# A two-block transformer kernel on one core: first modulation shared by VectorE and TensorE, the pool and part of the first projection moved beside the attention, and the expert choice fed from unnormed rows

## The chip, the core and the metric

The kernel runs on one core of a Trainium2 chip. The metric is the device time of one launch in microseconds (us), lower is better. Engines are named as the profile names them: PE is TensorE (PEld its weight loads), DVE is VectorE, ACT is ScalarE, POOL is GpSimd (it issues the indirect transfers here), SP is SyncE (it issues all other transfers).

## The reference, cut to what matters

Everything is float32; 256 tokens of 1024 columns, worked as two tiles (0 and 1) of 128 tokens.

```python
# first block
mod = silu(c) @ w_ada + b_ada                  # 1024 -> 6 * 1024, one row
sh_m, sc_m, gt_m, sh_f, sc_f, gt_f = split(mod, 6)
h = rms_norm(x, g_pre_mix) * (1 + sc_m) + sh_m
proj = h @ w_in                                # 1024 -> 2560: 256 pool columns, then q, k, v
pool = (banded_mean(proj[:, :256]) - proj[:, :256]) @ w_pool ...   # 4 groups of 64
attn = ...                                     # 3 dilations of 4 heads, 768 columns of q, k and v
y = concat(pool, attn) @ w_out
x = x + gt_m * rms_norm(y, g_post_mix)
h = rms_norm(x, g_pre_ffn) * (1 + sc_f) + sh_f
x = x + gt_f * rms_norm(conv_ffn(h), g_post_ffn)
# second block, twice (l = 0, 1)
x = x + mixer_l(rms_norm(x, attn_norm[l]))     # l = 0: two attentions with an index; l = 1: latent attention
h = rms_norm(x, ffn_norm[l])
q = (h @ w_q).reshape(s, 8 heads, 2, 128)      # product keys
sc = einsum(q, sub_keys)                       # 128 scores per head and half
top 16 of each half, 16 x 16 sums, top 16 of those -> 16 experts per head; g = softmax(top_s)
act = gelu(u[expert] . h)                      # rows of 1024 floats from a table of 16384
x = x + sum(g * act * v[expert])
# then a final rms_norm
```

## The kernel before, in words

`order()` writes one list of steps by hand; each engine's function walks that list and issues its own part of every step, so all queues are in order. PSUM is used as six banks in turn (`take`, L542): a step that fills a bank waits until its former reader (DVE or ACT, fixed in advance or by turns) has emptied it. Weights come through a ring of six slots of 1 MB (`weights`, L1582); a load waits until the slot's last reader is done, and all later loads wait behind it on SP.

The first modulation (`ada`, L57, L1136) works on chunks of 512 of the 6144 columns, in order 0 to 11. A chunk is two loads of 1 MB. DVE multiplies and adds its 8 blocks of 128 rows (L1146 once, L1148 seven times) into an accumulator, TensorE sums that over the partitions by a matmul with ones (`total`, L582), and DVE adds the bias, loaded as 128 copies (`finish`, L1160). Chunks 0 to 3 (sh_m and sc_m) come ahead of everything, with x, the bias of 2048 columns and the gain g_pre_mix loaded behind them. Then DVE takes the root of the mean square (`xscale`, L1174), folds 1 + sc_m with the gain (L1180), and modulates tile 0 (L1192, L1193) and, after the first 4 matmuls of the projection have been issued, tile 1. TensorE turns each tile by 8 transposes (L566), and `mm` (L605, matmul L621) multiplies: 5 column groups of `w_in`, 2 loads each, 2 tiles each. One 128x512 float32 matmul stands as two instructions in the profile. Chunks 4 to 7 lie between the steps of the projection, 8 and 9 in the attention, 10 and 11 in the up projection.

After the fifth column group comes the step `pool` (L632, L887, L1309): four band matmuls (L639), the transposes of q and k of both tiles (24 of them, L566), and the pool's matmul (L650). Then the eight attention units (`attention`, L84; 0 to 3 are tile 0, 4 to 7 tile 1): scores (L670), maximum on DVE (L1338), exp on ACT (L1020), transposes, values (L687). After the output projection (`wout`, L706), tile 0 is normed and added (`norm`, `add`, L1195, L1212), then tile 1, and then tile 0 is modulated (`modulate`, L1184) for the up projection (L753).

In the second block `choose` (L198) picks the experts of tile t in block l. The order is: sum of squares and root on ACT (L1001, L1004), Newton step and h on DVE (L1208, with the norm gain as 128 copies), 8 transposes of h (L566), 2 copies on ACT, 16 transposes of the sub-keys, then 4 column groups of w_q (L621, 8 k-steps each) with `qturn` (copy, 4 transposes, copy, score matmuls L808), and seven `pick` parts per group on DVE (L1440). ACT takes the exp of the 16 chosen scores. POOL then issues one indirect load per token tile and expert (`gather`, L1683, L1699), 512 KB each, 1024 of them, into 16 row buffers; a buffer is free when the dot product (L1537), the sum on TensorE (L825, L826) or the sum on DVE (L1556) has read it. `together` (L250) spreads the steps of the other mixers and choices between the experts by fixed costs.

Of the kernel before, what the change touches and what calls it, by code (L numbers as in the profile page):

```python
# [22 lines left out]

C_ID, C_MASK, C_FREQ, C_SGN, C_IOTA, C_END = 0, 128, 1152, 1264, 1376, 1392
# [25 lines left out]
def order():  # L50
# [6 lines left out]
    def ada():  # L57
        for i in range(12):
# [3 lines left out]
            if i not in (0, 4, 8, 10):  # L62
                put("total", i - 1)
            if i in (9, 11):
                yield
            if i in (3, 7, 9, 11):
                put("total", i)
                for n in range({3: 0, 7: 6, 9: 8, 11: 10}[i], i + 1):
                    put("finish", n)
            elif i in (5, 6):  # L70
                put("finish", i - 1)
            yield

    def projection(name, tiles):
        K, cols = PROJ[name[0]]
        for c in range(len(cols)):
            for k0 in range(0, K // 128, 4):
                for t in tiles:
                    put("mm", name, tiles, c, k0, t)
                    yield 0.85 * min(4, K // 128 - k0)  # L80
            for t in tiles:
                put("evac", name, c, t)

    def attention(name, units, cost):  # L84
        for u in range(units + 2):
            if u < units:
                put("score", name, u)
            if 1 <= u <= units:
# [7 lines left out]
    mods = ada()  # L96
    for _ in range(8):
        next(mods)
    put("xnorm")
    put("xscale")  # L100
    put("mod", "x0")
    win = projection(("win",), (0, 1))
    next(win)
    put("mod", "x1")
    put("angles")
    for n, _ in enumerate(win, 1):
        if n % 2 == 1 and n < 16:
            next(mods)
        if n == 14:
# [43 lines left out]

    def hybrid(t):
# [16 lines left out]
        yield from projection(("hyo", t), (t,))  # L171

    def mla(t):
# [22 lines left out]
        yield from projection(("mlo", t), (t,))  # L196
# [100 lines left out]
def program(nc, a, out):  # L297
    ctx = ExitStack()
    with ctx:
# [3 lines left out]
        def sem(name):  # L303
# [28 lines left out]
        l_first, l_cols, l_x, l_bias0, l_bias1, l_gains, l_tabs, l_pool, l_gains2 = (  # L332
            sem(n) for n in ("l_first", "l_cols", "l_x", "l_bias0", "l_bias1", "l_gains", "l_tabs", "l_pool", "l_gains2"))
# [14 lines left out]
        summed = sem("summed")  # L348
        held = sem("held")
# [1418 lines left out]
```

## Time and profile before

| what | us |
|---|---|
| median of 3 runs | 2113.08 |
| lowest, highest | 2112.03, 2113.08 |
| span of the profiled execution, first to last instruction | 2111.6 |

The page and the answers of the trace give the span of one execution only; the time of a run is longer than the span by what lies around the instructions, here 0.4 to 1.5 us if the profiled execution was like the timed ones. Times in rows count from the start of the span. "Idle before" in a row's brackets is the time for which the engine had nothing to do, and the arrow what ended it.

### The profile page before, as it was taken

What the parts mean: (1) busy time and instruction counts of PE and PEld (TensorE: products, weight loads), DVE (VectorE), ACT (ScalarE), POOL (GpSimd) and SP (SyncE); (2) the same over time, 40 slices, a digit from 0 to 9 for tenths busy, and PEclk for the clock granted to TensorE, in tenths of its full rate; (3) what the DMA queues carried; (4) which work ended last, traced back from release to release, by engine and by line L of the source; (5) the groups of instructions that cost most, each with busy time, mean ns of one, the idle gap of its engine ahead of it and who ended that gap; (6) DMA issues with size and microseconds to landing.
All of it is one profiled execution on the core that took longest, in us unless ns stands there. A gap on an engine that the chain in (4) does not pass through costs nothing.

```text
span 2111.6 us, 15758 instructions
## 1 busy us (share of the span) xinstructions
PE 1648.0 (78%) x4610; PEld 828.8 (39%) x4610; DVE 1375.4 (65%) x3269; ACT 388.8 (18%) x902; POOL 1128.4 (53%) x1028
## 2 busy tenths in 40 slices
PE   3997999998567978987876888878768996555565
PEld 1465887444233434432343433333434442111111
DVE  6564432142796695687757668776784887777775
ACT  1022000012121222222122222221322221100001
POOL 0000000000377577577766767776687777777773
PEclk9977999998789979999796999999788999887667
DMA  9851569162799999999999999999999999999997
GB/s 357 303 197 60 165 194 329 57 238 80 245 372 385 401 399 407 401 406 380 400 396 406 404 403 406 408 397 401 397 354 384 407 394 365 408 409 409 409 410 313
DMA packets 254483, 720.79 MB, mean 341 GB/s; under 512 B 24518, under 2 KB 49598, under 8 KB 253886
## 3 DMA queue, kind: packets, MB, share of 16 engines
q0 software_dynamic: 147456, 536.94, 65.0%
q1 hardware_dynamic: 106942, 182.85, 24.2%
q8 instruction: 38, 0.62, 0.1%
q14 instruction: 47, 0.39, 0.0%
HBM read 718.66 MB, written 1.05 MB: 341 GB/s over the span
## 4 chain that ended last, share of the span: by engine, by line
PE 40%; DMA 21%; POOL 17%; DVE 13%; issue 7%; ACT 2%; SPq 0%; POOLq 0%; DVEq 0%; ACTq 0%
POOL gring L1699 17%; DMA gring<-in_peer_v_dram,sel_idx 17%; PE PS L621 13%; PE PS L753 7%; PE PS L825 5%; PE PS L826 5%; DVE gring L1537 4%; PE PS L727 4%; PE PS L566 3%; DMA gring<-in_peer_u_dram,sel_idx 2%; DMA wring<-in_hyb_w_in_dram 1%; DVE xs L1556 1%; PE PS L670 1%; PE PS L687 1%; PE PS L706 1%
## 5 line engine op out<-in xcount | busy, mean ns | idle before, releaser
L1699 POOL DMA_INDIRECT gring<-in_peer_u_dram,sel_idx x512 | 566.0, 1105 | 725.1 <-DVE sel_g L1523 556.2
L825 PE MATMUL PS<-gring,diags 128*128 128x512 f32 x736 | 449.0, 695 | 321.3 <-DMA gring<-in_peer_v_dram,sel_idx 211.5
L1699 POOL DMA_INDIRECT gring<-in_peer_v_dram,sel_idx x512 | 562.2, 1098 | 230.3 <-issue 130.5
L1537 DVE CUSTOM_DVE_ANT_0 gring<-gring,hs 128x1024 f32<-128x1024 f32 x400 | 482.1, 1221 | 134.3 <-DMA gring<-in_peer_u_dram,sel_idx 133.1
L826 PE MATMUL PS<-gring,diags 128*128 128x512 f32 x736 | 434.2, 676 | 0.0
L621 PE MATMUL PS<-wring,hTs 128*128 128x512 f32 (+3 forms) x968 | 410.4, 574 | 9.8 <-DVE hTs L1125 4.3
L825 PEld LDWEIGHTS PS<-gring,diags 128*128 128x128 f32 x736 | 135.4, 210 | 545.4 <-issue 383.4
L621 PEld LDWEIGHTS PS<-wring,hTs 128*128 128x128 f32 x968 | 179.8, 195 | 219.8 <-issue 217.4
L826 PEld LDWEIGHTS PS<-gring,diags 128*128 128x128 f32 x736 | 158.8, 216 | 210.5 <-issue 210.5
L1063 ACT ACTIVATE diags<-consts,acts 128x128 f32<-128x128 f32 x368 | 136.4, 397 | 511.3 <-PE PS L826 476.8
L1537 DVE CUSTOM_DVE_ANT_0 gring<-gring,PS 128x1024 f32<-128x1024 f32 x112 | 136.4, 1220 | 70.4 <-DMA gring<-in_peer_u_dram,sel_idx 70.4
L753 PE MATMUL PS<-hTs,wring 128*128 128x256 f32 (+1 forms) x768 | 154.8, 365 | 1.9 <-DVE hTs L1101 1.9
L753 PEld LDWEIGHTS PS<-hTs,wring 128*128 128x128 f32 x768 | 137.5, 193 | 19.8 <-issue 2.3
L1556 DVE SCALAR_TENSOR_TENSOR xs<-gring,acts,xs 128x1024 f32<-128x1024 f32 x80 | 102.6, 1282 | 8.3 <-DMA gring<-in_peer_v_dram,sel_idx 8.1
L566 PE MATMUL PS<-consts,work 128*128 128x128 f32 (+1 forms) x344 | 67.2, 321 | 50.0 <-ACT work L1020 18.6
L950 ACT ACTIVATE work<-PS 128x512 f32<-128x512 f32 (+4 forms) x122 | 55.7, 463 | 222.0 <-PE PS L621 114.0
L1556 DVE SCALAR_TENSOR_TENSOR PS<-gring,acts,PS 128x1024 f32<-128x1024 f32 x62 | 79.9, 1288 | 12.3 <-DMA gring<-in_peer_v_dram,sel_idx 8.8
L566 PEld LDWEIGHTS PS<-consts,work 128*128 128x128 f32 (+1 forms) x344 | 48.5, 161 | 84.5 <-ACT work L1020 23.6
L1020 ACT ACTIVATE work<-work,small 128x128 f32<-128x128 f32 (+3 forms) x72 | 35.3, 490 | 226.2 <-DVE small L1345 226.2
L1148 DVE SCALAR_TENSOR_TENSOR gring<-wring,small,gring 128x512 f32<-128x512 f32 x84 | 63.1, 751 | 3.9 <-DMA wring<-in_w_ada_dram 1.1
L727 PE MATMUL PS<-gring,keep 128*128 128x512 f32 x120 | 55.0, 600 | 0.9 <-issue 0.9
L1338 DVE CUSTOM_DVE_ANT_0 work<-PS,consts 128x128 f32<-128x128 f32 (+1 forms) x72 | 25.5, 354 | 38.1 <-PE PS L670 37.4
(194 smaller groups left out, 1188.9 us busy)
## 6 DMA issues: line engine op xcount, KB each, us to landing
wring<-in_peer_w_q_dram SPq DMA_DIRECT2D x32, 1024.0 KB, 14.7
wring<-in_w_ada_dram SPq DMA_DIRECT2D x24, 1024.0 KB, 9.7
wring<-in_w_up_dram SPq DMA_DIRECT2D x44, 512.0 KB, 5.1
wring<-in_hyb_w_in_dram SPq DMA_DIRECT2D x20, 1024.0 KB, 8.3
wring<-in_w_in_dram SPq DMA_DIRECT2D x10, 1024.0 KB, 8.1
wring<-in_hyb_w_out_dram SPq DMA_DIRECT2D x8, 1024.0 KB, 19.2
gring<-in_peer_u_dram,sel_idx POOLq DMA_INDIRECT x512, 12.9
gring<-in_peer_v_dram,sel_idx POOLq DMA_INDIRECT x512, 13.4
```

Source lines behind the costliest of these rows:

```text
L566: ins = pe.e.transpose(ps[0:c, 128 * i:128 * i + 128], s, ident)
L621: ins = pe.e.matmul(ps, lhs(k), slot[s][:, k - k0, 0:n], start=(k == 0), stop=(k == kt - 1))
L727: ins = pe.e.matmul(ps, gT[:, k, 128 * t:128 * t + 128], slot[s][:, k % 4, :], start=(k == first), stop=(k == last))
L753: ins = pe.e.matmul(PS[:, 512 * b + 256 * j + c0:512 * b + 256 * j + c0 + n], slot[s][:, k % 4, off + 128 * j:off + 128 * j + 128], hT[:, ...
L825: pe.e.matmul(ybank[0], d, row[i % NG][:, 0:512], start=first, stop=last)
L826: pe.e.matmul(ybank[1], d, row[i % NG][:, 512:1024], start=first, stop=last).then_inc(summed, 1)
L950: return ac.e.activation(dst, src, ACT.Copy)
L1063: ac.e.activation(d, ident, ACT.Copy, scale=acts[:, c:c + 1]).then_inc(diag_ready, 1)
L1148: ins = e.scalar_tensor_tensor(ac, slot[s][:, k % 4, :], cact[:, k:k + 1], ac, ALU.mult, ALU.add)
L1537: e.tensor_tensor_reduce(row[i % NG], row[i % NG], hbank if (l, t) == (1, 1) and hd else h[t], 1.0, 0.0, ALU.mult, ALU.add, acts[:, c:c + ...
L1556: e.scalar_tensor_tensor(x[t] if in_x or (hd, j) == (7, 15) else vbank, row[i % NG], acts[:, c:c + 1], x[t] if in_x or (hd, j) == (0, 1) e ...
L1699: gp.e.indirect_dma_start(out=row[i % NG], out_offset=None, in_=table, in_offset=bass.IndirectOffsetOnAxis(ap=sel_idx[:, c:c + 1], axis=0) ...
```

## The change

1. The modulation's first four chunks are taken in the order 2, 3, 0, 1 (`ADA`). For these four, DVE takes rows 0 and 1 of each load's four blocks of 128 (2 of 4), and TensorE takes the other two as matmuls with the activated c broadcast over 128 columns (`cwide`), with the bias as a matmul of one row, all in the bank into which `total` adds DVE's part. The copies of the bias for these chunks are not loaded; one row of 8 KB is (`brow`).
2. Chunks 2 and 3 are multiplied with the gain straight from PSUM (`widen`), x is scaled with them, and the shift of chunks 0 and 1 is added from PSUM by halves (`shift`); each half of each tile is turned at once (`wT`), and a matmul waits for its half only.
3. `pool` is split into `pm`, `qk` and `py`. Only `qk` of tile 0 stands ahead of the attention; `pm`, `qk` of tile 1, the fifth column group of `w_in` for tile 1, and `py` stand in units 0 to 4.
4. Tile 0's modulation for the up projection stands ahead of tile 1's norm and add; both its copies go to ACT.
5. In `choose`, x itself is turned (`xT`), its first half already inside the mixer's output projection, and multiplied by the norm gain (a column per partition now) on the way out of PSUM. The w_q matmuls start without the norm; the root 1/rms goes into the exp's scale. The norm stands behind the first `qturn`, three quarters of the key transposes too.

```diff
+ADA = (2, 3, 0, 1, 4, 5, 6, 7, 8, 9, 10, 11)
     def projection(name, tiles):
+            now = tiles[:1] if (name[0], c) == ("win", 4) else tiles
...
-    mods = ada()
-    for _ in range(8):
-        next(mods)
+    for i in (2, 3):
+        for part in (0, 1):
+            put("ada", i, part)
+        put("total", i)
+        put("widen", i)
     put("xnorm")
     put("xscale")
-    put("mod", "x0")
+    for part in (0, 1):
+        put("ada", 0, part)
+    put("total", 0)
+    for t in range(2):
+        put("shift", 0, t)
+        put("wT", 0, t)
+    for part in (0, 1):
+        put("ada", 1, part)
+    put("total", 1)
+    for t in range(2):
+        put("shift", 1, t)
+    mods = ada()
     win = projection(("win",), (0, 1))
-    next(win)
-    put("mod", "x1")
+    for t in range(2):
+        next(win)
+        put("wT", 1, t)
...
-    put("pool")
-    for n, _ in enumerate(attention(("a1",), 8, 1.0)):
-        if n % 2 and n < 10:
+    put("qk", 0)
+    beside = {0: [("pm",)], 1: [("qk", 1)], 2: [("mm", ("win",), (0, 1), 4, 0, 1)],
+              3: [("mm", ("win",), (0, 1), 4, 4, 1), ("evac", ("win",), 4, 1)], 4: [("py",)]}
+    for n, _ in enumerate(attention(("a1",), 8, 1.0, beside)):
+        if n in (3, 4, 5, 7, 9):
             next(mods)
...
-                 ("sq", "y1"), ("norm", "y1"), ("add", "y1")):
+                 ("sq", "y1"), ("mod", "f0"), ("norm", "y1"), ("add", "y1")):
         put(*step)
-    put("mod", "f0")
...
+    def out_projection(name, t, l):
+        for n, units in enumerate(projection(name, (t,)), 1):
+            if n == 3:
+                put("xT", t, l, 0)
+            yield units
...
     def choose(t, l):
-        put("sq", f"c{t}{l}")
-        yield 2.0
-        put("norm", f"c{t}{l}")
-        yield 2.0
-        put("hT", f"c{t}{l}")
-        yield 1.0
-        put("hTe", f"c{t}{l}")
-        yield 1.0
-        put("keys", t, l)
...
                 put("mm", ("wq", t, l), (t,), g, k0, t)
                 yield 3.4
+                if (g, k0) == (0, 0):
+                    put("sq", f"c{t}{l}")
+                    put("xT", t, l, 1)
+                    put("keys", t, l, 0)
+                    yield 2.0
...
             put("qturn", t, l, g)
+            if g == 0:
+                put("norm", f"c{t}{l}")
+                for part in (1, 2, 3):
+                    put("keys", t, l, part)
+                yield 3.0
...
+            def ada(i, g):
+                if i >= 4:
+                    return
+                if g == 0:
+                    b, ps = take(("total", i), "vec")
+                    pe.wait_ge(l_brow, 16)
+                    pe.wait_ge(wide_ready, 1)
+                    pe.e.matmul(ps, ones[0:1, :], brow[:, 512 * i:512 * i + 512], start=True, stop=False)
...
+                for k in (2, 3):
+                    pe.e.matmul(PS[:, 512 * b:512 * b + 512], cwide[:, 2 * g + k - 2, :], slot[s][:, k, :], start=False,
+                                stop=False)
...
+            def xturn(t, l, half):
+                key, at = ("xT", t, l, 4 * half), 24 + 8 * l + 4 * half
+                ps = arrived(key)
+                freed(key, e.tensor_tensor(
+                    hT[:, 4 * half:4 * half + 4, 128:256], ps.rearrange("p (b q) -> p b q", q=128),
+                    norm_cols[:, at:at + 4].unsqueeze(2).to_broadcast([128, 4, 128]), ALU.mult))
...
+                mine = range(4) if i >= 4 else range(2)
...
+            def widen(i):
+                ps = arrived(("total", i))
+                ve.wait_ge(l_gain0, 16)
+                freed(("total", i), e.scalar_tensor_tensor(mod[:, 512 * i:512 * i + 512], ps, 1.0,
+                                                           gain[0][:, 512 * (i - 2):512 * (i - 2) + 512],
+                                                           ALU.add, ALU.mult))
+
+            def shift(half, t):
+                ps = arrived(("total", half))
+                so_far()
+                ht = h[t][:, 512 * half:512 * half + 512]
+                ins = e.tensor_tensor(ht, ps, ht, ALU.add)
...
-                ve.wait_ge(*done(e.scalar_tensor_tensor(sc_m, sc_m, 1.0, gain[0], ALU.add, ALU.mult)))
...
+                for t in range(2):
+                    done(e.scalar_tensor_tensor(h[t], x[t], norm_small("x")[7][:, t:t + 1], sc_m, ALU.mult, ALU.mult))
...
-                    ac.e.activation(ga, ga, ACT.Exp).then_inc(gate_exp, 1)
+                    ac.wait_ge(h_ready, h_n[f"c{t}{l}"])
+                    ac.e.activation(ga, ga, ACT.Exp, scale=root(t, l)).then_inc(gate_exp, 1)
...
             def ada(i, g):
                 weights(("ada", i, g), [(0, a["w_ada"][0], 512 * g, 4, 512 * i, 512)])
                 if (i, g) == (3, 1):
                     group(l_x, (x[0], a["x"][0, 0:128, :]), (x[1], a["x"][0, 128:256, :]))
-                    group(l_bias0, (mod[:, 0:2048], a["b_ada"][0, 0:2048].partition_broadcast(128)),
-                          (gain[0], a["g_pre_mix"][0].partition_broadcast(128)))
+                    group(l_gain0, (gain[0], a["g_pre_mix"][0].partition_broadcast(128)))
```

Of the three new or changed functions named `ada`, the first is TensorE's, the one with `mine` is VectorE's, the last is SP's; `xturn` as shown is VectorE's. The load group of (3, 1) is thus issued after four weight loads now, and after eight before. The tables of the rotary angles are loaded behind the first load of `w_in`.

## Rows read from the trace of the kernel before

**Rows 1.** the page: the span, and GB/s in 40 slices of it

```profile
span 2111.6 us, 15758 instructions
...
GB/s 357 303 197 60 165 194 329 57 238 80 245 372 385 401 399 407 401 406 380 400 396 406 404 403 406 408 397 401 397 354 384 407 394 365 408 409 409 409 410 313
```

**Rows 2.** busy by engine per stretch (us, count in brackets), clock, DMA share, GB/s

```profile
120.80:139.70 18.90, 16.42 (x102) 13.55 (x102) 13.42 (x51) 7.17 (x16) 0.00 (x0) 0.84 0.38 119
139.70:171.00 31.30, 31.15 (x117) 24.77 (x117) 19.94 (x63) 7.89 (x15) 0.00 (x0) 0.55 0.32 96
556.70:1000.00 443.30, 354.42 (x974) 166.03 (x974) 342.11 (x944) 100.58 (x231) 322.46 (x281) 0.91 1.01 390
1530.00:1800.00 270.00, 215.20 (x557) 97.91 (x556) 201.46 (x529) 63.27 (x144) 209.54 (x181) 0.94 1.00 381
```

**Rows 3.** chain of waits, opening and projection: start, length, what

```profile
20.17 13.85 DMA gains<-in_g_pre_mix_dram
34.11 2.48 DVE gring L1160 x4
...
41.78 1.98 PE PS L566 x8
44.62 5.47 PE PS L621 x8
...
51.84 24.27 PE PS L621 x56
...
91.56 13.73 PE PS L621 x32
```

**Rows 4.** timeline of the opening, all engines: start, length, what, idle before

```profile
2.43 0.33 SPq L1592 DMA_DIRECT2D keep<-in_attn_norm_dram  x1
...
8.74 0.49 DVE L1146 TENSOR_SCALAR gring<-wring,small 128x512 f32<-128x512 f32 x1 [3.23 <-DMA wring<-in_w_ada_dram]
9.26 5.48 DVE L1148 SCALAR_TENSOR_TENSOR gring<-wring,small,gring 128x512 f32<-128x512 f32 x7
...
14.80 2.07 PE L582 MATMUL PS<-gring,keep 128*128 128x512 f32 x2 [9.66 <-DVE gring L1148]
...
30.25 1.06 ACT L963 ACTIVATE hs<-xs 128x1024 f32<-128x1024 f32 x1 [26.34 <-DMA xs<-in_x_dram]
...
39.19 1.28 DVE L1192 SCALAR_TENSOR_TENSOR hs<-xs,small,gring 128x1024 f32<-128x1024 f32 x1
```

**Rows 5.** the stretches of the attention where the clock falls, columns as in Rows 2

```profile
129.00:134.00 5.00, 3.09 (x27) 2.61 (x26) 4.50 (x23) 1.79 (x5) 0.00 (x0) 0.96 0.01 2
134.00:167.00 33.00, 32.43 (x114) 26.12 (x113) 22.62 (x79) 7.92 (x17) 0.00 (x0) 0.50 0.32 96
```

**Rows 6.** timeline between output and up projection

```profile
192.02 0.16 DVE L1167 TENSOR_TENSOR small<-small 128x1 f32<-128x1 f32 x1
...
196.38 1.28 DVE L1192 SCALAR_TENSOR_TENSOR hs<-xs,small,gring 128x1024 f32<-128x1024 f32 x1
...
198.97 1.97 PE L566 MATMUL PS<-consts,hs 128*128 128x128 f32 x8 [8.61 <-DVE hs L1193]
```

**Rows 7.** chain of waits, first choice

```profile
517.73 0.70 DVE xs L1283
...
523.80 5.38 PE PS L566 x24
529.18 7.12 PE PS L621 x16
...
538.32 1.17 PE PS L808 x8
...
556.70 1.07 POOL gring L1699
```

**Rows 8.** the page's group of dot products, busy and mean ns

```profile
L1537 DVE CUSTOM_DVE_ANT_0 gring<-gring,hs 128x1024 f32<-128x1024 f32 x400 | 482.1, 1221 | 134.3 <-DMA gring<-in_peer_u_dram,sel_idx 133.1
```

**Rows 9.** one line's instructions: the gain multiply of the mixers, ns min/median/max

```profile
L1125 DVE TENSOR_TENSOR hTs<-PS,small x12: 674/691/692, 411.3 to 1439.7; 128x512 f32<-128x512 f32 x12
```

More of the change, by code:

```diff
@@ L57, in ada @@
     def ada():
-        for i in range(12):
+        for i in range(4, 12):
             put("ada", i, 0)
@@ L76, in projection, with attention @@
         for c in range(len(cols)):
+            now = tiles[:1] if (name[0], c) == ("win", 4) else tiles
             for k0 in range(0, K // 128, 4):
-                for t in tiles:
+                for t in now:
                     put("mm", name, tiles, c, k0, t)
                     yield 0.85 * min(4, K // 128 - k0)
-            for t in tiles:
+            for t in now:
                 put("evac", name, c, t)
-    def attention(name, units, cost):
+    def attention(name, units, cost, beside={}):
         for u in range(units + 2):
@@ L87, in attention @@
                 put("score", name, u)
+            for step in beside.get(u, ()):
+                put(*step)
             if 1 <= u <= units:
@@ L170, in hybrid @@
         put("obT", "hy", t)
-        yield from projection(("hyo", t), (t,))
+        yield from out_projection(("hyo", t), t, 0)
     def mla(t):
@@ L463, in program @@
                 loads.append((("mm", s[1], s[3], s[4]), 1))
-            elif s[0] == "keys":
-                loads.append((s, 1))
+            elif s[0] == "keys" and s[3] == 0:
+                loads.append((s[0:3], 1))
             elif s[0] == "wout":
@@ L684, in value @@
                     ready(("mm", ("hyi", t), 6, t))
+                if name[0] == "a1" and u % 4 == 0:
+                    for c in (3, 4):
+                        ready(("mm", ("win",), c, t))
                 b, ps = take(("value", name, u), "vec")
@@ L797, in keys @@
                 kv = wring[:, 2048 * s:2048 * s + 2048].rearrange("p (b c) -> p b c", b=16)
-                turn(("ky", t, l), [kv[:, i, :] for i in range(16)], "act")
-                w_free[("keys", t, l)] = (full[use[("ky", t, l, 12)][0]], use[("ky", t, l, 12)][1])
+                b, ps = take(("ky", t, l, 4 * part), "act")
+                for i in range(4):
+                    ins = pe.e.transpose(ps[:, 128 * i:128 * i + 128], kv[:, 4 * part + i, :], ident)
+                ins.then_inc(full[b], 1)
+                if part == 3:
+                    w_free[("keys", t, l)] = (full[b], use[("ky", t, l, 12)][1])
             def qturn(t, l, g):
@@ L1034, in index, with keys @@
                     freed(("index", t, g), ac.e.activation(q, ps[:, 0:nk], ACT.Relu))
-            def keys(t, l):
-                turned(("ky", t, l), 16, lambda i0, n: kyT[:, i0:i0 + n, :])
+            def keys(t, l, part):
+                key = ("ky", t, l, 4 * part)
+                ps = arrived(key)
+                freed(key, copy(kyT[:, 4 * part:4 * part + 4, :], ps.rearrange("p (b q) -> p b q", q=128)))
             def qturn(t, l, g):
@@ L1566, in expert @@
                     ins.then_inc(y_added, 1)
-            own = {"start": start, "ada": ada, "finish": finish, "xnorm": xnorm, "xscale": xscale, "norm": norm, "add": add,
+            own = {"start": start, "ada": ada, "finish": finish, "widen": widen, "shift": shift, "xnorm": xnorm, "xscale": xscale, "norm": norm, "add": add,
                    "angles": angles, "score": score, "value": value, "fold": fold, "up": up, "gfold": gfold,
@@ L1571, in vector_engine @@
             first = {"mod": modulate, "turn": attturn, "lin": mrope_key}
-            own.update({"columns": columns, "hTe": hturn_gain, "lin": linturn})
-            after = {"evac": evac, "pool": pool}
+            own.update({"columns": columns, "hTe": hturn_gain, "lin": linturn, "xT": xturn})
+            after = {"evac": evac, "py": py}
             for s in steps:
```

180 lines of the change are left out of this document (116 added, 64 removed).

## The prediction

> **What bounds the kernel now.** I read the page first: in the last three quarters of the span the transfers run at about 400 GB/s in every slice [rows 1]. The stretches say the same: from 556.70, where POOL issues its first indirect load [rows 7], the DMA share is 1.00 to 1.01 at 381 to 390 GB/s, with no engine full [rows 2]. So 1555 of 2111.6 us are bound by bytes which the change leaves alone, and an engine's time saved there is worth nothing by itself. All that comes ahead of 556.70 runs at a third or half of that rate [rows 1]: there the transfers wait for the work, and a microsecond saved starts the gathers a microsecond earlier. A gain of the change must be found there.
>
> Second, the chain of waits of the opening [rows 3]. The end of the modulation is set by the load of the gain, landed at 34.02; the adds and the modulation follow, tile 0 is turned at 41.78, the first matmul of the projection starts at 44.62, and the ninth only at 51.84, since tile 1 had to be modulated and turned in between. From there TensorE is the bound up to 120.8. In the attention it stays so: 16.42 busy of 18.90 us, then 31.15 of 31.30 [rows 2]. The clock granted from 134 to 167 is 0.50, the level of 1.2 GHz, after 5 us in which TensorE was busy for 3.09 [rows 5].
>
> Third, the first choice: from the last add at 517.73 to the first gather at 556.70 one thing follows another [rows 7].
>
> **The opening.** Loads land in the order of issue and by bytes: the first MB at 8.74 [rows 4], the gain at 34.02 [rows 3] as the end of 11.0 MB (8 weight loads of 1.05, x 1.05, bias 1.05, gain 0.52); that is 9.96 MB in 25.3 us, 0.394 MB per us. Now two small loads more stand in front, 0.35 us each by the nearest row [rows 4], and the gain ends 5.77 MB: 8.74 + 0.7 + 4.72 / 0.394 = 21.4. x ended before it here too (30.25) [rows 4]. The last weight load, (1, 1), lands at 32.0.
>
> DVE's share of a chunk falls from 0.5 + 7 x 0.785 = 6.0 to 2.9 us [rows 4]. But widen(2) needs the gain and stands ahead of chunk 3 in DVE's queue, so all behind it waits until 21.4. Then in turn: widen 0.8, chunk 3 2.9, total 2.07 (TensorE has had nothing for some 4 us, so I take the pair at the slow level [rows 4]), widen 0.8: 28.0. Mean square, root and Newton step 1.3 (36.59 to 39.19, less one product of 128x1024 [rows 3, 4]), two scalings of 1.3 [rows 4], chunk 0 2.9: 34.8. Total 1.0, two shifts of 0.7, turning the second 0.6: 37.8. Only now, as `wT` stands ahead of it in TensorE's queue, chunk 1: bias, 4 k-steps, total, 6 x 0.86 at 2.4 GHz (32 instructions in 13.73, two to a matmul [rows 3]): 43.0. The first matmul starts there, against 44.62; the weights of `w_in`, the next MB behind (1, 1), land at 34.7 and are no bound. The ninth instruction starts after 3.43 and a turning of 0.5, at 46.9 against 51.84. **4.9 us** won. The relief of DVE is real but mostly lost to the wait for the gain and to chunk 1 behind the turnings. The one-row bias matmul is in no row; it costs between nothing and the slow pair (2.07), I take 0.86 as its columns are those of any pair. The broadcast copies (2 x about 0.4) lie before 8.74.
>
> The Trainium skill (DMA: Bandwidth & Descriptors, "Queues, rings and completion order") says that completion is not FIFO per issuing engine. By that the gain could land beside x, up to 1.05 / 0.394 = 2.7 us earlier, and the sum would be 2088.8. The rows show landing in order, so it stays out of the sum.
>
> **Projection and attention.** The fifth column group of tile 1, 16 instructions or 6.9 us, leaves the projection and enters units 2 and 3. TensorE's sum over projection and attention is unchanged but for the idle time that it fills: 18.90 - 16.42 = 2.5 us [rows 2]. Against it, the turning of q and k now stands right behind the ropes and chunk 7 on DVE, which had 13.7 us of matmuls for cover and now 6.9: I price a wait of 1.0. DVE's own load in the attention grows by the pool's four small operations (1.7 us); with 13.42 of 18.90 and 19.94 of 31.30 busy it has room. Then the clock: dense matmuls in units 2 and 3 put off the fall which came at 134, and what of tile 0 ran slow may run at full: between 0 and 2.7 us for the 5.4 us from 134 to 139.7; I take 1.0. Unknown from both sides: if the moved matmuls themselves run at 1.2 GHz they cost 6.9 more; if units 4 to 7 ran at 2.4 GHz, TensorE's 31.15 would halve and DVE's 19.94 plus the pool's be the bound, some 8 us less. Sum 4.9 + 2.5 - 1.0 + 1.0 = **7.4 us** at the end of the attention.
>
> **Tile 0's modulation.** DVE has ended tile 0's Newton step at 192.18 and starts L1192 at 196.38, behind tile 1's norm and add [rows 6]. Moved ahead, TensorE's turning at 198.97 starts **4.2 us** earlier. Tile 1's norm and add move behind it by 2.5 us; its own turning is needed at the end of the first up step (9 us later), which covers them. Both copies on ACT instead of one: 0.6 behind the other, under the second half of the turning.
>
> **The first choice.** Before: add 517.73 to 518.43, squares, root, Newton, h, turning and keys from 523.80 (5.38), 16 instructions at 529.18 (7.12: part of them slow), copies and turning, scores from 538.32 to 539.49 [rows 7]. Now: the first half of x is turned inside the output projection (0.4 more on TensorE: 518.1). The first 8 instructions follow at once, the clock still up: 3.4, to 521.5. Turning of the second half 0.5, gain product 0.7 [rows 9], beside which lie the first 4 key transposes: 522.8. 8 instructions 3.4, then copy, turning, copy and scores as before (529.18 + 7.12 = 536.30 to 539.49, 3.2): 529.4. **10.0 us** won. The square, the table load and the root on ACT lie beside the first matmuls, the Newton step and h (2.5 us on DVE) beside the second and the copies; 12 key transposes beside DVE's picks. The exp takes the root as a scale, ready by 525. From the scores to the gather nothing changes (17.2 us).
>
> **The other three choices** lie in the stretch bound by bytes: nothing. There ACT loses 1.2 us of copies and DVE gains 1.4 each; the gathers' reserve covers it.
>
> **Sum.** 7.4 + 4.2 + 10.0 = 21.6 us: a span of 2111.6 - 21.6 = 2090.0. The median of the runs is 1.5 above that span, so the time is 2113.1 - 21.6 = **2091.5**.
>
> **The rivals.**
> *The clock stays low (0.11).* TensorE in the opening is fed in bursts of two k-steps and waits for each load. If it works at 1.2 GHz until 50, chunk 0's part ends after DVE's (27.2 + 8.6 + 2.1 = 37.9), chunk 1's six pairs take 10.3: the first matmul at 50, the ninth 10 us later than I say. With the moved matmuls partly slow (3.4) it gives 2105. For it: pairs of 2.07 all through the opening [rows 4], 33 us at 0.50 though busy [rows 5]. Against: of the 8 instructions in 5.47 us half already ran at full [rows 3]. The Trainium skill (TensorE: Matmul & The Clock Gate, "HAM oscillation") describes this rule: short bursts between waits for loads start slow every time. Rows 5 agree in part: the fall came after small work, with only short waits.
> *The attention speeds up (0.12).* Units 4 to 7 run mostly at 2.4 GHz: 8 us less, 2083.
> *The gathers profit too (0.07).* Slower stretches such as 1530 to 1800 (381 against 410 GB/s) hold choices; if earlier scores fill half of that, 9 us less: 2082.
> *Given back (0.09).* What the weight loads moved ahead of 556.70 they must now move behind it: at about 200 GB/s for 17 us of the gain, 3.4 MB or 8.5 us: 2100. Against: the ring of six slots is freed by the same matmuls, which come earlier too.
> *No measurable change (0.04).* Clock and giving back together: 2105 + 5 and more, near 2110.
> *Slower (0.05).* In the gathers' stretch TensorE's queue now meets DVE's three times in a choice (product of half 0, add and product of half 1) where it met it once (h); each may stand behind four dot products of 1.22 us [rows 8], and TensorE's sums, which free the row buffers, stand behind. Two more meetings at 4.9 us in three choices are 29 us; over 21.6 it decides, from 3.6 us a meeting. Time 2121. Against: 16 rows of 0.52 MB are 20 us of cover, and DVE is busy for 342 of 443 us.
>
> **How the numbers follow.** My own case has 0.52, with 2086 to 2097 by its bounds. All but the clock's, the unchanged and the slower case (0.20 together) lie between 2078 (the fast ones with the 2.7 of the gain and a little more) and 2103. What can be told from no change is 0.2%, 4.2 us, here. Faster 0.52 + 0.11 + 0.12 + 0.07 + 0.09 = 0.91, same 0.04, slower 0.05.
>
> **What would show it.** First matmul of the projection near 43 and the ninth near 47, DVE idle before the first widen until about 21; end of the values near 163.5; up projection near 190 instead of 201.9; first POOL load near 535; from there to the end 1555 again. I am wrong if the opening's pairs keep 2.07 after 30, if the clock digit in the moved matmuls is 5, or if the stretch behind the first gather is longer than 1560.

## The result, and the profile after

| | kernel before | kernel after |
|---|---|---|
| median of the first comparison, us | 2112.03 (5 runs, 2107.78 to 2113.08) | 2101.59 (5 runs, 2096.72 to 2102.72) |
| ratio, 95% interval | | 0.9948, 0.9930 to 0.9966 |
| mean of more runs, us | 2112.6 (74 runs, beside the experiments) | 2098.7 (11 runs, those five and six more) |
| profiled execution: time, span, us | span 2111.6 | 2096.72, span 2094.9 |

The change makes the kernel faster, by 10.4 us in the first comparison and by 13.9 us between the means of all runs. The forecast was 21.6 us. The same kernel spreads over some 10 us from run to run here (standard deviation 2.6 to 5.5 us), so means of many runs are used below, with one standard error behind a ±. In every run the time is 1.7 to 1.9 us above its span, 1.8 in what follows; the forecast had taken 1.5 for this.

The page after, the rows of [rows 1]:

```profile
span 2094.9 us, 15823 instructions
...
GB/s 339 307 198 61 221 179 292 115 182 116 301 397 383 401 401 403 401 406 401 395 395 407 400 404 406 369 391 401 399 382 399 408 364 363 410 409 410 409 410 308
```

The gathers' plateau begins about half a slice of 52 us earlier and looks as before. The opening, which answers to [rows 3], in the chain of waits (start, length, what):

```profile
9.41 11.91 DMA gains<-in_g_pre_mix_dram
...
21.45 0.69 DVE gring L1276
...
24.95 2.07 PE PS L638 x2
27.02 2.00 PE PS L624 x2
29.02 6.18 PE PS L629 x8
35.21 0.87 PE PS L638 x2
...
36.17 0.70 DVE hs L1284
...
36.92 1.25 PE PS L604 x8
38.17 1.05 PE PS L624 x2
39.22 3.63 PE PS L629 x8
42.85 0.86 PE PS L638 x2
43.71 3.43 PE PS L702 x8
...
47.58 3.44 PE PS L702 x8
```

Three readings: the gain lands at 21.32 instead of 34.02, and DVE does its first `widen` at 21.45; TensorE works at the slow level of its clock from 24.95 (2.07 for a pair of instructions) to about 35, though the prediction had given the slow level to one pair only; and chunk 1 (L624, L629, L638) stands between the first turnings and the first matmul of the projection (L702). The attention and the first choice, which answer to [rows 2] and [rows 7]; first the windows (busy us of PE, PEld, DVE, ACT, POOL with counts, then clock, DMA share, GB/s), then the chain:

```profile
120.80:139.70 18.90, 17.33 (x89) 11.68 (x87) 10.51 (x36) 3.53 (x8) 0.00 (x0) 1.00 0.65 222
139.70:171.00 31.30, 26.06 (x95) 19.49 (x96) 19.49 (x53) 7.21 (x13) 0.00 (x0) 0.62 0.33 102
```

```profile
510.82 0.70 DVE hTs L1240
511.66 3.69 PE PS L702 x8
...
517.36 1.17 PE PS L897 x8
518.55 0.90 DVE work L1583 x4
...
535.75 1.07 POOL gring L1826
```

Set beside the forecast:

| landmark, us | before | forecast | after |
|---|---|---|---|
| first matmul of the projection | 44.62 | 43.0 | 43.71 |
| ninth | 51.84 | 46.9 | 47.58 |
| tile 0 turned for the up projection | 198.97 | 187.4 | 187.31 |
| first POOL load | 556.70 | 535.1 | 535.75 |
| from there to the end | 1554.9 | 1555 | 1559.2 |

So the time in front of the gathers was forecast within 1 us, 21.0 measured against 21.6 (21.4 by the mean of two profiles). What is missing is missing behind them. By the mean of the runs the stretch behind is 2098.7 - 1.8 - 535.3 (mean of two profiles) = 1561.6 us for the kernel after and 2112.6 - 1.8 - 556.7 = 1554.1 for the one before: **7.5 us longer**, with a standard error of 1.3 from the runs alone and what one profile's start of the gathers may be off besides. The windows of the two stretches:

```profile
535.75:2094.90 1559.15, 1168.08 (x2854) 519.97 (x2854) 1139.46 (x2653) 310.24 (x730) 1135.40 (x1024) 0.87 1.01 392
```

and of the kernel before:

```profile
556.70:2111.60 1554.90, 1166.32 (x2854) 519.58 (x2854) 1136.62 (x2647) 311.76 (x736) 1128.21 (x1024) 0.87 1.01 393
```

Time by rate gives 611 MB on both sides. The only column that grows by more than 3 us is POOL's, by 7.2 us for the same 1024 instructions. Part of that is spread between executions: a second profile of the kernel after has 3.8 us less of both, stretch and POOL.

```profile
534.90:2090.30 1555.40, 1165.61 (x2854) 517.89 (x2854) 1139.62 (x2653) 310.14 (x730) 1131.63 (x1024) 0.88 1.01 393
```

### The profile page after: what moved, and what is told of

It is laid out like the page before. It is cut to its first block, busy times and chain, and to the rows that moved or that the text cites. A ratio compares the mean times of both kernels' runs of the same rounds, so it can differ in the third digit from the quotient of the medians.

```text
span 2094.9 us, 15823 instructions
## 1 busy us (share of the span) xinstructions
PE 1660.3 (79%) x4650; PEld 829.5 (40%) x4650; DVE 1364.9 (65%) x3261; ACT 386.4 (18%) x895; POOL 1135.6 (54%) x1028
## 3 DMA queue, kind: packets, MB, share of 16 engines
HBM read 717.63 MB, written 1.05 MB: 343 GB/s over the span
## 4 chain that ended last, share of the span: by engine, by line
PE 39%; DMA 19%; POOL 18%; DVE 14%; issue 8%; ACT 1%; SPq 0%; POOLq 0%; DVEq 0%; ACTq 0%
POOL gring L1826 18%; PE PS L702 12%; DMA gring<-in_peer_v_dram,sel_idx 12%; PE PS L838 7%; DMA gring<-in_peer_u_dram,sel_idx 5%; PE PS L914 5%; PE PS L915 4%; DVE gring L1661 4%; PE PS L812 4%; PE PS L604 2%; DMA wring<-in_hyb_w_in_dram 1%; DVE xs L1680 1%; PE PS L752 1%; PE PS L791 1%; PE PS L772 1%
## 5 line engine op out<-in xcount | busy, mean ns | idle before, releaser
L1826 POOL DMA_INDIRECT gring<-in_peer_u_dram,sel_idx x512 | 566.6, 1107 | 702.7 <-DVE sel_g L1647 535.3
L1826 POOL DMA_INDIRECT gring<-in_peer_v_dram,sel_idx x512 | 568.8, 1111 | 228.6 <-issue 126.9
L702 PE MATMUL PS<-wring,hTs 128*128 128x512 f32 (+3 forms) x968 | 411.4, 575 | 10.6 <-DVE hTs L1198 4.4
L702 PEld LDWEIGHTS PS<-wring,hTs 128*128 128x128 f32 x968 | 180.6, 196 | 221.9 <-issue 219.0
L1044 ACT ACTIVATE work<-PS 128x512 f32<-128x512 f32 (+2 forms) x123 | 56.2, 465 | 229.1 <-PE PS L702 92.9
L1258 DVE SCALAR_TENSOR_TENSOR gring<-wring,small,gring 128x512 f32<-128x512 f32 x68 | 51.1, 751 | 3.6 <-DMA wring<-in_w_ada_dram 1.5
## 6 DMA issues: line engine op xcount, KB each, us to landing
gring<-in_peer_u_dram,sel_idx POOLq DMA_INDIRECT x512, 11.7
```

The lines of the kernel that those rows point to most:

```text
L702: ins = pe.e.matmul(ps, lhs(k), slot[s][:, k - k0, 0:n], start=(k == 0), stop=(k == kt - 1))
L1044: return ac.e.activation(dst, src, ACT.Copy)
L1258: ins = e.scalar_tensor_tensor(ac, slot[s][:, k, :], cact[:, 4 * g + k:4 * g + k + 1], ac, ALU.mult, ALU.add)
L1826: gp.e.indirect_dma_start(out=row[i % NG], out_offset=None, in_=table, in_offset=bass.IndirectOffsetOnAxis(ap=sel_idx[:, c:c + 1], axis=0) ...
```

## The experiments

Each is timed beside the kernel before on the same chip. "Head" is the start of the first POOL load in its profile.

**The kernel after, again.** No edit.

> The changed kernel once more, on the chip of the next three. Its first profile had the first gather 20.9 us earlier and the end 16.7 us earlier than the kernel before, but the medians differ by only 10.4 us. If the stretch behind the first gather is truly longer, this run is again 9 to 12 us faster than the kernel before (ratio 0.994 to 0.996) with the first gather at 535 to 536 and 1559 us or more behind it. If the first comparison was unlucky, the ratio is 0.990 and the stretch 1555.

Median 2097.58, ratio 0.9931 (0.9912 to 0.9951), mean 15.1 ± 1.9 below the kernel before, head 534.90. The two theories are not parted by it: the ratio lies between theirs, and in its own profile the stretch behind the head is 1555.4 us, what "unlucky" asked for, but that execution took 2092.07 us, and by the mean of the six runs, 2097.4, the stretch is 1560.7. A part of the first comparison's shortfall was spread; by the means, not all.

**Parts undone or done alone.** Three kernels: the kernel after with the new choice only for the first one (tile 0, block 0), of whose edit the main lines come first below; the kernel after with no new choice at all (`NEW = ()`); and the kernel before with tile 0's modulation moved and nothing else (the last lines).

```diff
+NEW = ((0, 0),)
-            if n == 3:
+            if n == 3 and (t, l) in NEW:
                 put("xT", t, l, 0)
...
     def choose(t, l):
+        if (t, l) not in NEW:
+            put("sq", f"c{t}{l}")
...
-                 ("sq", "y1"), ("norm", "y1"), ("add", "y1")):
+                 ("sq", "y1"), ("mod", "f0"), ("norm", "y1"), ("add", "y1")):
```

> The changed kernel, with the new order of the expert choice for tile 0 of block 0 only; the three later choices in the old order, with normed rows. The first gather must stay at 535 to 536. Theory L (what is lost behind the first gather is lost in the reordered later choices: products and turnings between the w_q matmuls, the keys' load behind the first w_q load): the stretch behind it is 1555 again and the time 2091 to 2093, ratio 0.990. Theory H (a part of any gain ahead of the first gather is given back behind it): as fast as the changed kernel, 2100 to 2102, ratio 0.995. Theory N (no loss, it is spread between runs): 2091 to 2102 with no clear difference from the changed kernel.

> The changed kernel with all four choices in the old order: only the opening, the pool and attention, and the modulation of tile 0 are changed. From my own sum the first gather is at 545.5 (the choice's 10.0 us are gone, of 20.9). Theory L: all of the 10.9 us arrive, 2101 to 2102, ratio 0.995, so as fast as the whole change. Theory H: half arrives, 2106 to 2107, ratio 0.9975.

> The kernel before with one step moved: tile 0's modulation for the up projection ahead of tile 1's norm and add. My price is 4.2 us: the turning at 194.8 instead of 198.97, the first gather at 552.5. If a microsecond ahead of the gathers counts in full: 2107.8 to 2108.8, ratio 0.998. Theory H: 2110, ratio 0.999. If the 4.2 us are taken back by tile 1's turning (late because its norm and add now stand behind), the first gather stays at 556.7.

| kernel | head | head against 556.70 | mean time against before | ratio (interval) |
|---|---|---|---|---|
| later choices as before | 536.41 | -20.3 | -16.1 ± 2.1 | 0.9930 (0.9914, 0.9946) |
| no new choice | 545.02 | -11.7 | -6.4 ± 1.2 | 0.9969 (0.9955, 0.9983) |
| tile 0's modulation only | 553.72 | -3.0 | -4.8 ± 1.4 | 0.9978 (0.9963, 0.9992) |

The first choice counts in full: from the second row to the first the head gains 8.6 us and the time 9.7 ± 2.2. So does the moved modulation, within its error. The order in the three later choices makes no difference that these runs can tell (-16.1 and -15.1). But between the last two rows lie 8.7 us of head and only 1.6 ± 1.8 us of time: what the opening and the part beside the attention win seems to be lost again.

**Whose turn it is to copy.** Copies out of PSUM without a fixed engine go to ACT, and every fourth to DVE. The change takes six banks fewer by turns ahead of the second block, so this turn falls on other copies behind it. The counter is set on by two in the kernel after, and in the kernel before.

```diff
                 taken[2] = 4
+                taken[1] += 2 * (t == 0)
```

> The changed kernel takes six PSUM banks fewer by turns (the turnings of both tiles for the first projection and of tile 0 for the up projection have a fixed reader now), so from the second block on, where every fourth such bank goes to VectorE, the turn falls two places apart from the kernel before. Here a 2 is added to the counter at that point, so that the same copies go to VectorE as before; nothing else is changed. Theory P (the shifted turns make the stretch behind the first gather longer): first gather still at 535 to 536, mean time 5 to 7 us below the changed kernel, 2092 to 2094. Theory R (what is missing at the end is only the spread of the runs) and theory H (a part of any gain is given back): as the changed kernel, mean 2098 to 2099.

> The kernel before with the turn of the copies moved by two places at the same point, so that they fall as in the changed kernel. Theory P: first gather unchanged at 556.7, mean time 5 us above the kernel before, near 2117. Theories R and H: no difference from the kernel before.

The kernel after with the old turns: ratio 0.9917 (0.9901 to 0.9932), mean -18.2 ± 1.9, head 534.21; the kernel before with the new: ratio 1.0001 (0.9987 to 1.0015), mean +0.5 ± 1.4, although its one profile has the head at 560.45, 3.75 later. The first lies 3.1 ± 2.7 further below the kernel before than the kernel after did (-15.1), which by itself parts nothing. The second does not lose the 5 us that the turns were to cost, so they do not explain the loss. Its head moved without the time, which I can't explain; one profile's head may be a few us off the mean of the runs.

**The gain first.** The load of the gain stands ahead of the weight loads.

```diff
+                group(l_gain0, (gain[0], a["g_pre_mix"][0].partition_broadcast(128)))
                 group(l_cols, (cw[0:66, :], a["conv_w"][0].rearrange("t (j c) -> (t j) c", c=128)),
...
-                    group(l_gain0, (gain[0], a["g_pre_mix"][0].partition_broadcast(128)))
```

> The changed kernel with the gain's load ahead of the weight loads instead of behind x. VectorE's first widen then does not wait for it (21.4 in the changed kernel) but for TensorE's sum of chunk 2, near 17.4; next it waits for the root of the mean square, which hangs on x landing at 20 to 21.5. From the rows of the changed kernel: scalings end near 28.7 instead of 31.6, first matmul of the projection at 40.2 instead of 43.6, first gather 3.4 us earlier, 532. If instead the second chunk of TensorE or the last weight load is what binds the opening, the first matmul stays at 43. The time follows by 3 us if gains ahead of the gathers count in full.

Head 533.33, mean 16.3 ± 2.4 below before, ratio 0.9930 (0.9910 to 0.9950): no gain over the kernel after that can be told. The chain of waits says why:

```profile
32.02 0.70 DVE hs L1284
...
32.76 1.97 PE PS L604 x8
...
36.73 6.39 PE PS L629 x8
43.13 0.86 PE PS L638 x2
43.98 3.43 PE PS L702 x8
```

The shift starts 4.2 us earlier (32.02 against 36.17), but TensorE has had nothing for 2.8 us before the total of chunk 0, and then does chunk 1 at the slow level: 8 instructions of L629 take 6.39 instead of 3.63, and the projection starts at 43.98, later than the 43.71 without the edit.

**The part beside the attention undone; the opening alone.** The first is the kernel after, with the pool, tile 1's turnings and its fifth column group ahead of the attention again. The second also has the old choice and the old place of tile 0's modulation: of the change the opening is left, with some small things of the kernel after that were not undone (where chunks 4 to 7 stand between the steps of the projection, when the rotary tables are loaded, both copies of the turned f0 on ACT, a wait ahead of the exp of the choices, the turns of the copies).

```diff
-            now = tiles[:1] if (name[0], c) == ("win", 4) else tiles
+            now = tiles
...
+    put("pm")
     put("qk", 0)
+    put("qk", 1)
+    put("py")
...
-    for n, _ in enumerate(attention(("a1",), 8, 1.0, beside)):
-        if n in (3, 4, 5, 7, 9):
+    for n, _ in enumerate(attention(("a1",), 8, 1.0)):
+        if n % 2 and n < 10:
```

> The changed kernel with its third part undone: the pool, tile 1's turnings and tile 1's fifth column group stand ahead of the attention again. What I forecast for that part is 2.5 - 1.0 + 1.0 = 2.5 us: the first gather then starts at 535.8 + 2.5 = 538.3, and the time is about 2101 (changed kernel, mean of 11 runs 2098.7). Rival, from the three undone parts so far (the choice and tile 0's modulation counted in full, what is left, opening and third part, moved the first gather by 8.7 us and the time by 1.6): the third part costs something behind the first gather, and without it the time is no longer, 2096 to 2099, though the first gather is later.

> The kernel before with the opening alone (shared modulation, gain earlier, shift by halves). Its first gather should come 4.4 us earlier (the ninth matmul instruction of the projection was at 51.84 and is at 47.42), at 552.3. If the opening counts in full, the mean lies 4.4 below the mean of the kernel before in the same batch; if it is the opening that is lost behind the first gather, at 0 to 1 below.

The first: head 540.21, 4.9 us later than the kernel after (535.3) where I had priced the part at 2.5; mean -12.2 ± 2.2, ratio 0.9943 (0.9923 to 0.9964), 1.6 us slower than the kernel after with an error of 2.4, which excludes neither the forecast nor its rival. The second: head 554.03, ratio 1.0005 (0.9992 to 1.0017), mean +0.6 ± 1.1. **The opening alone brings nothing that can be told.** Its head is 2.7 us earlier, not 4.4: chunk 1 took 5.33 us here for what took 3.63 in the profile of the kernel after:

```profile
37.53 1.05 PE PS L641 x2
38.58 5.33 PE PS L646 x8
43.91 0.86 PE PS L655 x2
44.76 3.43 PE PS L721 x8
```

By this one profile's head that leaves 3.3 ± 1.1 us that go lost behind it, though the opening moves no work there.

**Chunk 1's matmuls earlier.** TensorE does its share of chunk 1 before the total of chunk 0, and the total and the shift of chunk 1 stand behind the first matmuls of the projection (`adaP` is TensorE's share alone, `ada` for chunk 1 then VectorE's and the load); once with the gain where it was, once with the gain first.

```diff
     for part in (0, 1):
         put("ada", 0, part)
+    for part in (0, 1):
+        put("adaP", 1, part)
     put("total", 0)
...
     for part in (0, 1):
         put("ada", 1, part)
-    put("total", 1)
-    for t in range(2):
-        put("shift", 1, t)
...
-    for t in range(2):
-        next(win)
-        put("wT", 1, t)
+    next(win)
+    put("total", 1)
+    for t in range(2):
+        put("shift", 1, t)
+    next(win)
+    for t in range(2):
+        put("wT", 1, t)
```

> The changed kernel with TensorE's share of chunk 1 (bias row and 4 k-steps) ahead of the total of chunk 0, so ahead of the turnings, and the total and shift of chunk 1 behind the first matmuls of the projection. My working said that chunk 1 behind the turnings costs 6 x 0.86. By that the first matmul of the projection starts at 39 instead of 43.55 and its 17th instruction near 47.8 instead of 51.3: first gather 3.5 us earlier, 532.3, time 3.5 below the changed kernel's mean of 2098.7, 2095. Rival (clock): TensorE runs these matmuls at the slow level while it waits between loads, the 17th instruction starts later than 50 and the gain is under 1.5 us.

> As the run before it, and the gain loaded ahead of the weights as well. Alone the earlier gain brought the first gather forward by only some 2 us, as chunk 1 then ran at the slow level behind the turnings. With chunk 1 ahead of them TensorE is idle for less: first matmul of the projection at 35.5 (bound by its own weights, which land near 35), 17th instruction near 44.5, first gather near 529.0, time near 2092. Rival (clock): the first 16 instructions of the projection take 2 us a pair instead of 0.86, about 8 us more than I say for them; then nothing is won over the run before, 2095 or later.

The first is a miss: head 536.74, mean -13.0 ± 1.7, ratio 0.9945 (0.9928 to 0.9963). TensorE works at the slow level after its wait before 24.88 (3.77 us), as the kernel after does, and now the matmuls of both chunks stand ahead of the total of chunk 0, which starts 5 us later:

```profile
24.88 2.08 PE PS L643 x2
26.95 2.00 PE PS L629 x2
28.95 6.63 PE PS L634 x8
35.59 1.05 PE PS L629 x2
36.64 3.63 PE PS L634 x8
40.27 0.87 PE PS L643 x2
```

The second is the fastest kernel of the study, faster than both: median **2089.15, ratio 0.9902 (0.9886 to 0.9919)**, mean -22.1 ± 1.4, head 531.28. The timeline of TensorE (its brackets: idle before, and what ended it):

```profile
23.24 1.98 PE L634 MATMUL PS<-wring,diags 128*128 128x512 f32 x4 [0.68 <-DMA wring<-in_w_ada_dram]
25.96 1.98 PE L634 MATMUL PS<-wring,diags 128*128 128x512 f32 x4 [0.74 <-DMA wring<-in_w_ada_dram]
27.88 1.12 PE L629 MATMUL PS<-keep 1*128 1x512 f32 x2
...
31.37 1.98 PE L634 MATMUL PS<-wring,diags 128*128 128x512 f32 x4 [0.46 <-DMA wring<-in_w_ada_dram]
33.19 1.02 PE L643 MATMUL PS<-gring,keep 128*128 128x512 f32 x2
35.07 1.25 PE L607 MATMUL PS<-consts,hs 128*128 128x128 f32 x8 [0.85 <-DVE hs L1289]
36.50 3.67 PE L707 MATMUL PS<-wring,hTs 128*128 128x512 f32 x8 [0.18 <-ACT hTs L1049]
```

With the gain out of its way TensorE, from 16 us on, never waits for more than 0.85 us and stays at the full level; up to 33 its waits are for weights alone, and the projection starts at 36.50. Neither edit did it alone: each left TensorE idle for microseconds (2.8 and 3.8) and then paid in clock what it had won or could have won. Against the kernel after the head is 4.0 us earlier and the mean time 8.2 ± 1.7 lower, so about half of what this kernel wins lies behind the head, and no run shows why.

**The kernel after, held up.** Is the stretch behind the head longer because it begins earlier, or because of the new code? Here the kernel after is held up until it starts its first gather as late as the kernel before.

```diff
                 ps = arrived(key)
+                for _ in range(28 if (t, l, half) == (0, 0, 1) else 0):
+                    ve.wait_ge(*done(e.tensor_tensor(
+                        hT[:, 4:8, 128:256], ps.rearrange("p (b q) -> p b q", q=128),
+                        norm_cols[:, at:at + 4].unsqueeze(2).to_broadcast([128, 4, 128]), ALU.mult)))
```

> The changed kernel with its first choice held up: the gain product of the second half of tile 0 is done 29 times over instead of once, 28 x 0.74 = 20.7 us, so that the first gather starts at 556 to 560, where the kernel before starts it. Everything else is the changed kernel's. Over the runs so far the time gives back about a quarter of what the first gather gains (weighted slope 0.75). Theory one, it is the starting time itself (a microsecond earlier is worth 0.75): the time rises by 0.75 x 21 = 15.7 over the changed kernel and comes out at the time of the kernel before, within 1.5 of its mean in this batch. Theory two, it is the new code, whose stretch behind the first gather is 6 to 7 us longer wherever it starts: the time rises by the full 21, 5 to 7 us above the kernel before.

```profile
529.71 0.70 DVE hTs L1244
530.55 5.47 PE PS L702 x8
...
556.42 1.07 POOL gring L1830
```

Head 556.42, the same as before's 556.70; time 2117.7 in the mean against 2111.2 beside it, 6.5 ± 1.3 slower, ratio 1.0031 (1.0017 to 1.0046). Against the undelayed kernel it is 18.9 ± 1.6 us slower for 21.1 us of delay. Theory one wanted it within 1.5 us of the kernel before and fails; theory two holds: **at this place a microsecond in front of the gathers is worth about one, and the new code costs about 6.5 us behind them also when it starts where the old one does.** In its own profile the stretch is 1557.8 us.

## Why the prediction was right and wrong

- **"A gain of the change must be found" ahead of 556.70: right.** The held-up kernel, the choice and the moved modulation all pay about one for one. The opening's 2.7 us, alone, did not show in the time.
- **The opening, 4.9 us: 4.3 in the profile** (ninth matmul instruction at 47.58). The wait for the gain until 21.4 came as worked out. The slow level took more than I gave it (from 24.95 to about 35 instead of one pair; chunk 0's eight instructions 6.18 us, so the sign of being wrong that I had named for the opening came in part), but most of that work lay beside DVE's share of chunk 0; the bias row at 0.86 came as 1.05. It leans on the clock: in the opening alone the same instructions of chunk 1 took 5.33 instead of 3.63, and the head came 2.7 earlier.
- **Projection and attention, 7.4 in all: 7.7** at the end of the values (170.96 and 163.30). The idle time was filled (17.33 busy instead of 16.42 in the first window) and the clock there was 1.00 instead of 0.84; it fell all the same afterwards, 0.62 in the second. Undoing this part cost 4.9 us of head where its terms had 2.5, so the split between it and the opening was off, the sum was not.
- **Tile 0's modulation, 4.2: 4.0** in the profile of the kernel after (7.7 at the values, 11.7 at the turning for the up projection); 3.0 of head alone.
- **The first choice, 10.0: 10.2** (21.0 at the gather less 10.8 at the last add before the choice, 517.73 and 506.95).
- **"The other three choices ... nothing": not refuted.** Undone, they change nothing that can be told; the slower case (two more meetings of TensorE with DVE in a choice, 29 us) did not come.
- **"From there to the end 1555 again": this step failed.** The sum of 21.6 took the stretch behind the first gather as bound by bytes and so as untouched. It has the same bytes, and in the mean of the runs it is 7.5 us longer, 6.5 at an equal start. With the 0.2 us that the head came short of its forecast, that is all of the difference between the 21.6 forecast and the 13.9 measured. The bound of 1560 that I had named is passed by the mean (1561.6), not by the two single profiles (1559.2 and 1555.4), which shows how little one profile says at this size. So 2101.59 lies outside the 2086 to 2097 of my own case, and inside the whole range only because that was widened for the rivals.
- **"Given back", at 2100, had the right size and the wrong mechanism**: the bytes behind the head are the same 611 MB within the rounding of the rates (some 1 MB), where this rival had 3.4 MB more.
- **Small slips of the working:** from 134 to 139.7 are 5.7 us, not 5.4; and the clock rival priced a slow pair at 1.72 (twice 0.86) where the rows read have 2.07 and the kernel after 2.00 to 2.07. Nothing in the sum hangs on either.

What makes the stretch longer is not settled. Excluded or not supported are: bytes, the earlier start, the order in the later choices, whose turn it is to copy. The kernel with the opening alone carries 3.3 ± 1.1 of it, by one profile's head. The mean time less 1.8 less the head gives 1557.4 to 1562.9 for the ten kernels that have the new opening, and 1552.2 to 1554.1 for the three that have not (the kernel before, that with tile 0's modulation moved, that with the new turns). So the opening is a suspect, but no more: all ten are built from the kernel after and the three from the kernel before, and the kernel after with the old opening was not run, so the small things that were not undone are a rival that stands. Nor do the profiles part the two groups by themselves: span less head is 1549.4 to 1563.0 in the eleven profiles of kernels with the new opening (mean 1556.5) and 1550.0 to 1554.9 in the other three (mean 1552.6). What would act hundreds of microseconds later was not found. Where in time it lies can be said: from the start of the 224th gather from the end to that of the last it is 277.8 us before, 277.2 after and 278.9 in the held-up kernel, so the difference arises ahead of them, where other work lies beside the gathers.

## What to carry to other kernels

Where only the head's start was moved (the first choice, the held-up kernel), a microsecond of it paid about one; what the opening won did not show by itself, so the time and not the head has the last word. A stretch bound by bytes at a DMA share of 1.00 is not therefore constant, and a forecast of 1% needs an allowance for it of the size of the spread of its runs. In an opening fed by loads, look for TensorE's waits of several microseconds before counting columns: take the input that stalls its queue out of the way and put independent matmuls into the waits, together, since each alone may only move the stall and lose its gain in the clock. Time the parts one by one: here one of the largest edits, the opening, brought nothing by itself that could be told.

## What the runs showed of the hardware

**The indirect load's issue stretches beside some operations of DVE.** One instruction of POOL takes 0.94 us when DVE is idle (117 of the 1024 in the kernel after) and up to 2.0 beside DVE, but not beside all of its work. It goes by where DVE's inputs lie. Beside a dot product of a gathered row with h in PSUM and nothing else, 108 issues all took 0.93 to 0.95 us; beside one with h in SBUF (`hs`), 203 issues took 1.25 in the mean and up to 2.00. In the other 13 profiles it is the same: at most 0.95 there, 1.20 to 1.24 in the mean and 1.98 or more at most here. A dip of the kernel after (window from 1700 to 1720) and its tail (from 1900), in the windows' row and the timeline:

```profile
1700.00:1720.00 20.00, 14.12 (x39) 5.74 (x38) 13.18 (x26) 4.74 (x10) 16.04 (x14) 1.00 0.89 317
1900.00:1920.00 20.00, 12.49 (x16) 3.84 (x16) 14.41 (x21) 2.10 (x6) 15.12 (x17) 0.66 1.03 410
```

```profile
1708.54 1.22 DVE L1661 CUSTOM_DVE_ANT_0 gring<-gring,hs 128x1024 f32<-128x1024 f32 x1
1708.58 1.99 POOL L1826 DMA_INDIRECT gring<-in_peer_u_dram,sel_idx  x1 [0.30 <-issue]
...
1904.21 1.22 DVE L1661 CUSTOM_DVE_ANT_0 gring<-gring,PS 128x1024 f32<-128x1024 f32 x1
1904.59 0.94 POOL L1826 DMA_INDIRECT gring<-in_peer_v_dram,sel_idx  x1 [0.30 <-issue]
```

In the dip POOL issues without a pause but the 0.30 us between two instructions, and 14 gathers of 0.52 MB touch the 20 us; the transfers run at 317 GB/s with a share of 0.89, while in the tail, where DVE is as busy (14.41 us), 17 gathers keep them at 410. So in such places POOL's issue and not the bytes is what is full, and what DVE does beside it can change the length of the stretch. This fits POOL's 7.2 us more in the longer stretch, but no run here changed it alone, and the second profile of the kernel after has half of these 7.2 us without any edit, so as the cause it is only argued. The Trainium skill (SBUF — State Buffer, "Who interferes with whom") says that a DVE instruction with at most one input in SBUF, outside the two-port modes, does not contend with GpSimd, that one with two inputs in SBUF contends with a GpSimd instruction that reads SBUF, and it infers that `tensor_tensor` all the same leaves descriptor generation alone. The rows agree with the first (108 issues of 0.93 to 0.95). With the inference they do not agree: these dot products have two inputs in SBUF, and the issues beside them are the long ones.

**The clock can fall in waits and stay low while busy.** TensorE had nothing for 4.2 us before 24.95 in the kernel after; the windows of that kernel, of the fastest one, and of the one with the opening alone, columns as above:

```profile
24.95:34.20 9.25, 9.25 (x11) 3.19 (x12) 6.41 (x13) 0.20 (x1) 0.00 (x0) 0.50 1.05 388
```

```profile
16.00:46.00 30.00, 26.75 (x69) 11.06 (x70) 16.77 (x29) 5.31 (x9) 0.00 (x0) 1.00 1.05 390
```

```profile
38.50:42.00 3.50, 3.50 (x6) 1.44 (x6) 2.40 (x4) 0.00 (x0) 0.00 (x0) 0.54 1.05 390
```

In the first, for over 9 us of gapless work the granted clock was 0.50, the level of 1.2 GHz, and then rose. In the second, with waits of at most 0.85 us, it was 1.00 for 30 us. But short waits alone do not keep it up: in the third it fell in chunk 1 although the waits since the clock had risen (near 32) were only 0.36 and 0.85 us, and that is the 5.33 us for chunk 1 above.
